# Delta inverse in a two-block kernel: the innermost level moved to VectorE, first phases as 64x64 tiles, bias rows, modulation and a table load moved

## The chip, the cores and the metric

One core of one Trainium2 chip. The time is that of one execution on the device, in microseconds. The kernel before ran three times: 841.18, 842.73 and 843.54, median 842.73. The profiled execution took 843.59. The profile calls the engines PE (TensorE's matmuls), PEld (its weight loads), DVE (VectorE), ACT (ScalarE), POOL (GpSimd) and SP (the engine that issues most DMAs).

## The reference

256 tokens of width 1024 pass through two blocks. The first is a gated delta-rule layer and an attention layer with shared keys and values. The second is a retention layer and a chunked attention layer, each with shift, scale and gate vectors (the "modulation") made from a condition vector. The change sits in the delta rule and around it. Cut to that:

```python
# per head, tokens in 4 chunks of 64
decay = exp(where(tril, g[:, None] - g[None, :], -inf))
a_mat = where(strict, (k * beta) @ k.T * decay, 0)         # 64 x 64, strictly lower
sol   = triangular_solve(a_mat + eye(64), [v * beta, k * beta * exp(g)])
# then a scan over the chunks: v_new = u - w @ state; o = q_dec @ state + qk @ v_new; ...
# second block: mod = silu(c) @ ada_w + ada_b ;  h = rms_norm(x) * (1 + scale) + shift
# attention: bias[h, i, j] = table[h, clip(i - j)]  added to the scores
```

## The kernel before, in words

**Weights.** All weight matrices stream in as 112 chunks of 1 MB (128 x 8 x 256 fp32) into three buffers `raw`. ACT rounds each half chunk to fp32r (`high`, tile `whi`), DVE makes the remainder (`low`, tile `wlo`), and PE multiplies three times per tile: high x high, high x low, low x high. One such job of 48 matmuls makes 256 output columns; the jobs are numbered J. SP loads chunk c once DVE has split chunk c - 3.

**The delta inverse.** Two chunks of 64 tokens lie side by side in a 128 x 128 matrix, so 8 heads make 16 matrices (`nt` holds minus a_mat, transposed). The inverse of each unit triangular matrix is built level by level, from blocks of 1 to blocks of 64 (`LEVELS` is 7, levels 0 to 6). The 32 x 32 blocks on the diagonal stand in `tt32`, their transposes in `uu32`. A level below 5 has two phases on PE: `first_products` (off-diagonal part times left inverse, into PSUM), an ACT copy of the result into `xs32`, and `second_products` (right inverse times that). Then DVE's `take_rows` writes the new entries into `tt32` with `copy_predicated` under the mask `lmask` and transposes the whole into `uu32`. Each phase is 64 small fp32 matmuls, 16 matrices times four 32 x 32 tiles, and a fp32 matmul runs as two records with a weight load each. Level 5 joins blocks of 32 (`take_halves`), level 6 joins blocks of 64 with 64 x 64 tiles and then transposes the 16 matrices.

**The order around it** is written out by hand on every engine. On PE, jobs 8 to 15 of the first projection are cut into `parts`, and a level lv takes this form: first products, a few transposes, `parts(J, 0, 4)`, second products, `parts(J, 4, 8)`, with J = 9 + lv. Four parts are 24 matmuls. The parts are meant to run while ACT and DVE work on a level. Each engine takes its instructions strictly in order and waits on semaphores (`t_ok` for a finished level, `x_ok` and `xc_ok` for the first phase and its copy, `u_ok` for the copies of level 6).

**The modulation.** `pair_sums(n)` on DVE multiplies a 1 MB piece `ada_ring` by the condition vector in eight passes; PE then sums over the partitions (`ada`), and DVE adds the bias (`mod_of_slot`, `take_mod`). SP loads the next piece when the one before is used up. `pair_sums(0)` stands on DVE in level 5, behind `low(15)` and ahead of `take_halves`.

**The bias rows.** POOL writes two small tables 32 times each into DRAM (`bias_rows_d`, 1 MB, and `bias_rows_b`, 512 KB), to read them back skewed as attention bias tiles. The sources `fd` and `fb` lie in `early`, memory that the outputs `ohi` and `olo` take over, so DVE waits for both writes (`scr_out`) before the delta outputs.

**The start.** ACT squares the input, then loads the table set for Ln and Exp (`ln_exp_set`), splits chunk 0 and computes the first norm. PE runs dummy matmuls (`keep_warm`) in the meantime.

## Time and profile before

| what | value |
|---|---|
| runs | 841.18, 842.73, 843.54 us; median 842.73 |
| profiled execution | 843.59 us, of which the profile's span is 841.7 |
| PE busy | 813.3 us, 97% |
| PEld / DVE / ACT / POOL busy | 791.7 / 601.6 / 488.8 / 41.1 us |
| chain that ended last | PE 83%, DVE 7%, DMA 4%, ACT 3%, issue 2% |
| PE jobs of 48 matmuls, one matmul with 256 columns | x1024 at 283 to 288 ns, overlapped |
| instruction queue | 60 packets, 0.98 MB |

A busy PE is one with a matmul in flight, so the 97% leaves some 28 us in which it had none. An idle time is put down to what ended it; "issue" means that the engine waited for nothing that the profile shows. All times in the rows are microseconds from the start of the span, unless marked ns.

### The profile page before, as it was taken

Reading aid. Unit: us, or ns where it says so; the run is one execution under the profiler, and the core shown is the slowest. Engines: PE = TensorE matmul, PEld = TensorE weight load, DVE = VectorE, ACT = ScalarE, POOL = GpSimd, SP = SyncE. Lnnn points to the kernel's source line nnn. Section 1 sums busy time; section 2 is a strip of 40 time slices with the busy share of each in tenths; the row PEclk is TensorE's granted clock in tenths of the full one; section 3 lists DMA queues with packets and bytes.
Section 4 is the critical chain, followed back from the end, with each engine's and each line's share of the span. In section 5 each row is a group of like instructions: output and inputs, shape, how many; then the busy total and the mean of one; then the engine's idle time right before and its main releaser. Section 6 shows DMA issues by size and latency. Waiting matters only on the chain.

```text
span 841.7 us, 18018 instructions
## 1 busy us (share of the span) xinstructions
PE 813.3 (97%) x7646; PEld 791.7 (94%) x7646; DVE 601.6 (71%) x1045; ACT 488.8 (58%) x762; POOL 41.1 (5%) x63
## 2 busy tenths in 40 slices
PE   7999989699999999999999999999999999999998
PEld 7899979689999999999999999999999999999998
DVE  4786865478898787796888895655777877565662
ACT  5756547355665665664444454347777767777731
POOL 0500000006300000000000000200000000000000
PEclk9999999799999999999999999999999999999999
DMA  7362236642976664467666673892465444444450
GB/s 285 122 236 100 103 104 135 144 151 77 266 270 231 239 219 165 149 216 280 207 229 239 232 259 141 213 288 102 166 235 201 167 174 160 151 152 150 150 176 26
DMA packets 26495, 153.82 MB, mean 183 GB/s; under 512 B 2848, under 2 KB 3376, under 8 KB 12080
## 3 DMA queue, kind: packets, MB, share of 16 engines
q1 hardware_dynamic: 24432, 146.37, 49.7%
q0 software_dynamic: 1984, 6.31, 4.2%
q8 instruction: 60, 0.98, 0.5%
q14 instruction: 19, 0.16, 0.1%
HBM read 150.04 MB, written 2.62 MB: 181 GB/s over the span
## 4 chain that ended last, share of the span: by engine, by line
PE 83%; DVE 7%; DMA 4%; ACT 3%; issue 2%; SPq 0%; DVEq 0%; ACTq 0%
PE ps L484 82%; DMA raw<-weights 4%; DVE wlo L1423 2%; ACT whi L1006 1%; PE ps L862 1%; DVE early L1490 1%; DVE early L1594 1%; DVE ada_ring L1504 1%; PE ps L714 0%; DVE hlo L1451 0%; DVE arena L1455 0%; ACT L995 0%; DVE olo L1468 0%; ACT hhi L1036 0%; ACT arena L1196 0%
## 5 line engine op out<-in xcount | busy, mean ns | idle before, releaser
L1423 DVE TENSOR_TENSOR wlo<-raw,whi 128x1024 fp32r<-128x1024 f32 x224 | 267.1, 1229 | 120.6 <-ACT whi L1006 120.6
L484 PE MATMUL ps<-hhi,whi 128*128 128x256 f32 x1024 | 295.1, 288 | 7.1 <-DVE hlo L1449 2.8
L484 PE MATMUL ps<-hlo,whi 128*128 128x256 f32 x1024 | 290.3, 283 | 1.1 <-issue 1.1
L484 PE MATMUL ps<-hhi,wlo 128*128 128x256 f32 x1024 | 290.2, 283 | 0.0
L1006 ACT ACTIVATE whi<-raw 128x1024 fp32r<-128x1024 f32 x224 | 227.5, 1055 | 87.3 <-PE ps L484 60.9
L484 PEld LDWEIGHTS ps<-hhi,whi 128*128 128x128 f32 x1024 | 196.5, 192 | 10.2 <-issue 7.9
L484 PEld LDWEIGHTS ps<-hlo,whi 128*128 128x128 f32 x1024 | 196.7, 192 | 1.8 <-issue 1.3
L484 PEld LDWEIGHTS ps<-hhi,wlo 128*128 128x128 f32 x1024 | 196.6, 192 | 0.0
L484 PE MATMUL ps<-ohi,whi 128*128 128x256 f32 x448 | 128.8, 288 | 1.4 <-DVE olo L1468 1.2
L484 PE MATMUL ps<-olo,whi 128*128 128x256 f32 x448 | 126.7, 283 | 0.0
L484 PE MATMUL ps<-ohi,wlo 128*128 128x256 f32 x448 | 126.7, 283 | 0.0
L484 PEld LDWEIGHTS ps<-ohi,whi 128*128 128x128 f32 x448 | 85.9, 192 | 2.8 <-issue 2.0
L484 PEld LDWEIGHTS ps<-olo,whi 128*128 128x128 f32 x448 | 85.9, 192 | 0.5 <-issue 0.5
L484 PEld LDWEIGHTS ps<-ohi,wlo 128*128 128x128 f32 x448 | 85.9, 192 | 0.0
L484 PE MATMUL ps<-arena 128*128 128x256 f32 (+2 forms) x496 | 77.7, 308 | 4.4 <-DVE arena L1605 3.4
L484 PEld LDWEIGHTS ps<-arena 128*128 128x128 f32 (+1 forms) x496 | 70.2, 191 | 10.9 <-DVE arena L1605 3.6
L484 PE MATMUL ps<-whi,hhi 128*128 128x256 f32 x256 | 72.6, 284 | 0.0
L484 PE MATMUL ps<-whi,hlo 128*128 128x256 f32 x256 | 72.4, 283 | 0.0
L484 PE MATMUL ps<-wlo,hhi 128*128 128x256 f32 x256 | 72.4, 283 | 0.0
L1504 DVE SCALAR_TENSOR_TENSOR ada_ring<-ada_ring,sil 128x256 f32<-128x256 f32 x144 | 59.0, 480 | 0.0
L484 PEld LDWEIGHTS ps<-whi,hhi 128*128 128x128 f32 x256 | 49.0, 192 | 0.7 <-issue 0.4
L484 PEld LDWEIGHTS ps<-whi,hlo 128*128 128x128 f32 x256 | 49.0, 192 | 0.3
(227 smaller groups left out, 953.7 us busy)
## 6 DMA issues: line engine op xcount, KB each, us to landing
raw<-weights SPq DMA_DIRECT2D x112, 1024.0 KB, 4.9
ada_ring<-ada SPq DMA_DIRECT2D x24, 1024.0 KB, 5.1
arena<-bias_rows_d POOLq DMA_DIRECT2D x4, 512.0 KB, 14.9
x<-x_t SPq DMA_DIRECT2D x2, 512.0 KB, 4.6
bias_rows_d<-early POOLq DMA_DIRECT2D x1, 1024.0 KB, 12.0
arena<-bias_rows_b POOLq DMA_DIRECT2D x4, 256.0 KB, 8.0
arena<-bias_rows_d POOLq DMA_DIRECT2D x4, 256.0 KB, 17.2
out_t<-x SPq DMA_DIRECT2D x4, 256.0 KB, 2.4
```

Source lines behind the costliest of these rows:

```text
L484: return pe.matmul(o, l, r, start=start, stop=stop, skip_group_check=skip)
L862: m = pe.transpose(turned_bank(hh, soft0)[:, a * P:a * P + P], ts[:, hh, c0:c0 + P], ident)
L1006: act.activation(whi[:, unit % UNITS, :, :], raw[:, c % RAW, 4 * half:4 * half + 4, :], ACT.Copy).then_inc(hi_ok_sem, 1)
L1423: dve.tensor_tensor(wlo[:, unit % UNITS, :, :], raw[:, c % RAW, 4 * half:4 * half + 4, :], whi[:, unit % UNITS, :, :].bitcast(F32), ALU.su ...
L1490: m = dve.scalar_tensor_tensor(out=dst[:, t, c0:S], in0=bank(J)[:, t, 0:S - c0], scalar=col("conv", 4 * tile + j), in1=dst[:, t, c0:S], op ...
L1504: own(dve.scalar_tensor_tensor(out=b, in0=b, scalar=sil[:, k:k + 1], in1=ring[:, :, k - 2, :], op0=ALU.mult, op1=ALU.add))
L1594: m = dve.copy_predicated(T, lmask[block_of(i), lv, :].rearrange("p (a b) -> p a b", b=n), ps[2 + i][block_of(i), 256:512].rearrange("p (a ...
```

## The change

It has six parts.

1. **Level 0** has no matmuls any more. With blocks of 1 the new entries are entries of `nt` itself, so DVE copies the superdiagonal of every 2 x 2 block into `uu32` (`next_to_diagonal`, two calls), and one transpose makes `tt32`. POOL prepares `uu32` instead of `tt32` and makes level 0's mask from the identity.
2. **First products of levels 1 to 4** run on two 64 x 64 tiles instead of four 32 x 32 tiles. For that ACT copies the 32 x 32 diagonal blocks of `nt` into a zeroed tile `ntm` (`own_blocks`), and its copies into `xs32` become two of 64 partitions instead of four of 32.
3. **Level 5 and the modulation.** On DVE `pair_sums(0)` and `take_halves` go ahead of `low(15)`, and `mod_of_slot(0)` comes into level 5. On PE `ada(0)` moves from level 6 into level 5.
4. **Bias rows.** `bias_rows_b` is written after the copies of level 6 (`u_ok` 4) instead of after level 4. The table `fd` moves from `early` into `turns`, and `bias_rows_d` is written only after ACT's sines in the second layer. DVE's wait for the writes moves behind the first output's product and waits for `bias_rows_b` alone.
5. **Table load.** `ln_exp_set()` moves ahead of the wait for the input.
6. **Keep-warm.** 20 and 12 dummy matmuls instead of 16 and 8.

```diff
+        ntm = A(16384, 16, 64)
...
-        fd = early[0:16, 0:512]
+        fd = turns[0:16, 0:2, :].rearrange("p a b -> p (a b)")
...
-                pool.tensor_copy(tt32[block_of(i), :, :], ident[block_of(i), block_of(i)].unsqueeze(1).to_broadcast([32, 16, 32])).then_inc(tt_ok_sem, 1)
+                pool.tensor_copy(uu32[block_of(i), :, :], ident[block_of(i), block_of(i)].unsqueeze(1).to_broadcast([32, 16, 32])).then_inc(tt_ok_sem, 1)
             pool.wait_ge(tt_ok_sem, 4)
-            pool.wait_ge(conv_ok_sem, 1)
+            pool.memset(ntm[:, :, :], 0.0).then_inc(ntm_zero_sem, 1)
             pool.tensor_copy(tt[:, :, :], ident.unsqueeze(1).to_broadcast([P, 16, P])).then_inc(tt_ok_sem, 1)
...
-            pool.dma_start(fd[:, 127:384], rel_d).then_inc(rel_d_in_sem, 16)
-            pool.wait_ge(rel_d_in_sem, 16)
-            pool.tensor_scalar(fd[:, 0:127], fd[:, 127:254], 0.0, fd[:, 127:128], ALU.mult, ALU.add).then_inc(fd_ok_sem, 1)
-            pool.tensor_scalar(fd[:, 384:512], fd[:, 255:383], 0.0, fd[:, 383:384], ALU.mult, ALU.add).then_inc(fd_ok_sem, 1)
-            pool.wait_ge(fd_ok_sem, 2)
-            pool.wait_ge(t_ok_sem, 5)
-            pool.dma_start(scr_d[0:32].rearrange("p h t -> h p t"), fd[:, :].unsqueeze(1).to_broadcast([16, 32, 512])).then_inc(scr_out_sem, 16)
             pool.wait_ge(bias_sb_sem, 1)
+            pool.wait_ge(u_ok_sem, 4)
             pool.dma_start(scr_b[0:32].rearrange("p h t -> h p t"), fb[0:8, :].unsqueeze(1).to_broadcast([8, 32, 512])).then_inc(scr_out_sem, 16)
             pool.wait_ge(o_split_sem, 4)
             pool.wait_ge(pos_in_sem, 16)
...
-            pool.wait_ge(scr_out_sem, 32)
+            pool.wait_ge(scr_out_sem, 16)
...
+            pool.wait_ge(fin_rope_sem, 3)
+            pool.dma_start(fd[:, 127:384], rel_d).then_inc(rel_d_in_sem, 16)
+            pool.wait_ge(rel_d_in_sem, 16)
+            pool.tensor_scalar(fd[:, 0:127], fd[:, 127:254], 0.0, fd[:, 127:128], ALU.mult, ALU.add).then_inc(fd_ok_sem, 1)
+            pool.tensor_scalar(fd[:, 384:512], fd[:, 255:383], 0.0, fd[:, 383:384], ALU.mult, ALU.add).then_inc(fd_ok_sem, 1)
+            pool.wait_ge(fd_ok_sem, 2)
+            pool.dma_start(scr_d[0:32].rearrange("p h t -> h p t"), fd[:, :].unsqueeze(1).to_broadcast([16, 32, 512])).then_inc(scr_out_sem, 16)
+            pool.wait_ge(scr_out_sem, 32)
...
-            keep_warm(16)
+            keep_warm(20)
             sums(lambda t: xsq_a[:, 4 * (t // 2) + t % 2, :], 4, S, sq_ok_sem, lambda t: t // 2 + 1)
-            keep_warm(8)
+            keep_warm(12)
...
-            parts(9, 0, 1)
...
-            def first_products(lv, c0):
-                left = left_of(lv) if lv < 5 else lambda v: v
-                n = 16 if lv < 5 else 32
-                for m16 in range(16):
...
-                    for k, r in steps_of(lv):
-                        m = mm(ps[2 + k][block_of(r), o], nt[block_of(k), m16, block_of(r)], left(tt32[block_of(k), m16, :]), m16 == 0, True)
+            parts(9, 0, 8)
+            def first_products(lv):
+                if lv < 5:
+                    left = left_of(lv)
+                    for m16 in range(16):
+                        o = slice(16 * m16, 16 * m16 + 16)
+                        for h in range(2):
+                            m = mm(ps[2 + h][half_of(h), o], ntm[half_of(h), m16, :], left(tt32[half_of(h), m16, :]), m16 == 0, True)
+                else:
+                    for m16 in range(16):
+                        o = slice(32 * m16, 32 * m16 + 32)
+                        for k in (0, 2):
+                            m = mm(ps[2 + k][block_of(k + 1), o], nt[block_of(k), m16, block_of(k + 1)], tt32[block_of(k), m16, :], m16 == 0, True)
                 return m
...
-            def second_products(lv, c0):
-                n = 16 if lv < 5 else 32
+            def second_products(lv):
+                n, c0, rows = (16, 256, range(4)) if lv < 5 else (32, 0, (1, 3))
                 for m16 in range(16):
                     o, i = slice(c0 + m16 * n, c0 + m16 * n + n), slice(m16 * n, m16 * n + n)
-                    for _, r in steps_of(lv):
+                    for r in rows:
                         m = mm(ps[2 + r][block_of(r), o], uu32[block_of(r), m16, :], xs32[block_of(r), i], m16 == 0, True)
                 return m
-            pe.wait_ge(nt_ok_sem, 4)
-            pe.wait_ge(tt_ok_sem, 4)
-            first_products(0, 256).then_inc(tp_ok_sem, 1)
-            parts(9, 1, 8)
...
                 pe.wait_ge(t_ok_sem, lv)
+                if lv == 1:
+                    pe.wait_ge(ntm_ok_sem, 2)
...
                 else:
-                    first_products(lv, 0).then_inc(x_ok_sem, 1)
+                    first_products(lv).then_inc(x_ok_sem, 1)
...
-                if last:
+                parts(J, 0, 4)
+                if lv == 5:
                     ada(0, taken(slot_of_mod(0)))
-                parts(J, 0, 4)
...
+            ln_exp_set()
             act.wait_ge(x_in_sem, 32)
             for t in range(4):
                 act.activation(xsq_a[:, 2 * t:2 * t + 2, :], x[:, 2 * t:2 * t + 2, :], ACT.Square).then_inc(xsq_ok_sem, 1)
-            ln_exp_set()
...
+            def own_blocks(m0, m1):
+                act.wait_ge(nt_ok_sem, m1 // 4)
+                for i in range(4):
+                    c = 32 * (i % 2)
+                    m = act.activation(ntm[block_of(i), m0:m1, c:c + 32], nt[block_of(i), m0:m1, block_of(i)], ACT.Copy)
+                m.then_inc(ntm_ok_sem, 1)
+            act.wait_ge(ntm_zero_sem, 1)
+            own_blocks(0, 12)
+            own_blocks(12, 16)
             first_tap(8)
             high(10)
...
                     act.wait_ge(x_ok_sem, lv)
-                    n = 256 if lv < 5 else 512
-                    for k, r in steps_of(lv):
-                        m = act.activation(xs32[block_of(r), 0:n], ps[2 + k][block_of(r), 0:n], ACT.Copy)
+                    for h in range(2):
+                        if lv < 5:
+                            m = act.activation(xs32[half_of(h), 0:256], ps[2 + h][half_of(h), 0:256], ACT.Copy)
+                        else:
+                            m = act.activation(xs32[block_of(2 * h + 1), :], ps[2 + 2 * h][block_of(2 * h + 1), :], ACT.Copy)
                     m.then_inc(xc_ok_sem, 1)
...
-            pair_matrices(3)
             dve.wait_ge(tt_ok_sem, 4)
             dve.wait_ge(mask_ok_sem, 5)
+            def next_to_diagonal(m0, m1):
+                dve.wait_ge(nt_ok_sem, m1 // 4)
+                for i in range(4):
+                    odd = lambda v: v.rearrange("p m (a two) -> p m a two", two=2)[:, :, :, 1]
+                    m = dve.copy_predicated(odd(uu32[block_of(i), m0:m1, :]), lmask[block_of(i), 0, 16 * m0:16 * m1].rearrange("p (m a) -> p m a", a=16),
+                                            odd(nt[block_of(i), m0:m1, block_of(i)]))
+                return m
+            next_to_diagonal(0, 12)
+            pair_matrices(3)
+            next_to_diagonal(12, 16).then_inc(u32_ok_sem, 1)
+            dve.wait_ge(u32_ok_sem, 1)
+            dve.transpose(tt32[:, :, :].rearrange("p m c -> p (m c)"), uu32[:, :, :].rearrange("p m c -> p (m c)")).then_inc(t_ok_sem, 1)
             def take_rows(lv):
-                dve.wait_ge(tp_ok_sem, lv + 1)
+                dve.wait_ge(tp_ok_sem, lv)
                 n = 1 << lv
...
-            take_rows(0)
...
-                low(10 + lv)
                 if lv < 5:
+                    low(10 + lv)
                     take_rows(lv)
                 else:
                     dve.wait_ge(sil_ok_sem, 1)
                     pair_sums(0)
                     take_halves()
+                    low(10 + lv)
+                    mod_of_slot(0)
                 if lv <= 3:
                     conv(8 + lv)
             pair_sums(1)
-            mod_of_slot(0)
             for g in range(4):
-                dve.wait_ge(tp_ok_sem, LEVELS - 1 + g + 1)
+                dve.wait_ge(tp_ok_sem, LEVELS - 2 + g + 1)
                 dve.tensor_copy(uu[0:64, 4 * g:4 * g + 4, 64:P], ps[2 + g][0:64, 256:512].rearrange("p (a b) -> p a b", b=64)).then_inc(u_ok_sem, 1)
             low(16)
...
-            dve.wait_ge(scr_out_sem, 32)
...
                 own(dve.tensor_tensor(oof[:, :, :], oof[:, :, :], zt[:, 2 * i:2 * i + 2, :], ALU.mult))
+                if i == 0:
+                    dve.wait_ge(scr_out_sem, 16)
                 split_o(oof[:, :, :], 2 * i, 2).then_inc(o_split_sem, 1)
```

What the order of the instructions shows on two engines. First VectorE, from level 4's rows taken to the end of level 6. In the names `wlo` is a weight remainder, `ada_ring` the modulation's piece. Before:

```order
L1594 COPY_PREDICATED early<-lmask,ps 32x16x16 x4
L1598 STREAM_TRANSPOSE early<-early 128x512
L1423 TENSOR_TENSOR wlo<-raw,whi 128x1024 x2
L1501 TENSOR_SCALAR ada_ring<-ada_ring,sil 128x2x128 x2
L1504 SCALAR_TENSOR_TENSOR ada_ring<-ada_ring,sil 128x2x128 x6
L1513 TENSOR_TENSOR ada_sum<-ada_ring 128x256
L1605 COPY arena<-ps 32x16x32 x2
L1501 TENSOR_SCALAR ada_ring<-ada_ring,sil 128x2x128 x2
```

And in the changed kernel:

```order
L1629 COPY_PREDICATED early<-lmask,ps 32x16x16 x4
L1633 STREAM_TRANSPOSE early<-early 128x512
L1522 TENSOR_SCALAR ada_ring<-ada_ring,sil 128x2x128 x2
L1525 SCALAR_TENSOR_TENSOR ada_ring<-ada_ring,sil 128x2x128 x6
L1534 TENSOR_TENSOR ada_sum<-ada_ring 128x256
L1640 COPY arena<-ps 32x16x32 x2
L1444 TENSOR_TENSOR wlo<-raw,whi 128x1024 x2
L1547 TENSOR_TENSOR mod<-ps,columns 128x2
```

The remainders of chunk 15 moved from ahead of the sums of the modulation to behind the copy that ends level 5.

Then TensorE, the small matmuls of levels 0 to 2 with their weight parts between them left out (24 matmuls each). Rows with 32x16 write 32 rows by 16 columns. Before:

```order
L484 MATMUL ps<-early,arena 32x16 x64
...
L484 MATMUL ps<-early,arena 32x16 x64
L721 MATMUL ps<-cst,arena 128x128 x8
...
L484 MATMUL ps<-early 32x16 x64
...
L484 MATMUL ps<-early,arena 32x16 x64
L731 MATMUL ps<-cst,early 128x128 x4
```

And in the changed kernel:

```order
L489 MATMUL ps<-early,arena 64x16 x32
L728 MATMUL ps<-cst,arena 128x128 x8
...
L489 MATMUL ps<-early 32x16 x64
...
L489 MATMUL ps<-early,arena 64x16 x32
L738 MATMUL ps<-cst,early 128x128 x4
...
L489 MATMUL ps<-early 32x16 x64
```

One group of 64 is gone, and the first group of each level is 32 instead of 64. The second groups are as they were.

## Rows read from the trace of the kernel before

**Rows 1.** Page: clock in 40 slices; the instruction queue (packets, MB).
```profile
PEclk9999999799999999999999999999999999999999
...
q8 instruction: 60, 0.98, 0.5%
```

**Rows 2.** PE timeline: start us, busy us, what [idle before it <-releaser].
```profile
106.63 0.39 PE L484 MATMUL ps<-hlo,whi 128*128 128x256 f32 x1 [1.13 <-issue]
...
110.90 0.25 PE L484 MATMUL ps<-early,arena 32*32 32x16 f32 x8 [1.94 <-issue]
...
121.83 0.70 PE L484 MATMUL ps<-early,arena 32*32 32x16 f32 x62 [0.80 <-issue]
...
136.86 0.31 PE L484 MATMUL ps<-early 32*32 32x16 f32 x16 [0.34 <-issue]
...
152.38 3.25 PE L484 MATMUL ps<-arena 64*64 64x64 f32 x32 [3.36 <-DVE arena L1605]
...
159.75 3.46 PE L714 MATMUL ps<-cst,arena 128*128 128x128 f32 x15 [3.73 <-issue]
```

**Rows 3.** Windows from stall end to stall end; (x) counts records.
```profile
106.62:110.89 4.27, 2.34 (x128) 2.11 (x128) 4.20 (x9) 0.00 (x0) 0.00 (x0) 1.00 0.44 182
136.85:159.74 22.89, 15.80 (x254) 14.92 (x254) 9.49 (x18) 10.29 (x19) 1.42 (x2) 0.85 0.84 152
```

**Rows 4.** Windows: a low-clock stretch, and the two bias-row writes.
```profile
112.00:115.40 3.40, 3.40 (x18) 3.40 (x18) 1.23 (x1) 3.34 (x9) 0.00 (x0) 0.50 0.02 5
139.70:151.70 12.00, 9.31 (x185) 8.76 (x183) 6.49 (x14) 7.87 (x14) 1.38 (x2) 1.00 0.85 91
151.70:162.20 10.50, 6.10 (x45) 5.42 (x46) 0.62 (x1) 2.72 (x6) 0.00 (x0) 0.56 0.76 163
```

**Rows 5.** DMA issues landing around 139 to 163 us: KB each, us to landing.
```profile
bias_rows_d<-early POOLq DMA_DIRECT2D x1, 1024.0 KB, 12.0
...
raw<-weights SPq DMA_DIRECT2D x1, 1024.0 KB, 15.8
bias_rows_b<-early POOLq DMA_DIRECT2D x1, 512.0 KB, 21.8
```

**Rows 6.** Timeline of DVE around level 5.
```profile
146.31 1.23 DVE L1423 TENSOR_TENSOR wlo<-raw,whi 128x1024 fp32r<-128x1024 f32 x1 [5.43 <-ACT whi L1006]
...
150.93 1.39 DVE L1605 COPY arena<-ps 32x512 f32<-32x512 f32 x2
```

**Rows 7.** Groups by shape, 87 to 170: busy, mean ns | idle.
```profile
L1594 DVE COPY_PREDICATED early<-lmask,ps 32x256 f32<-32x256 uint8 x20 | 11.1, 553 | 6.9 <-PE ps L484 6.7
```

**Rows 8.** DVE timeline: the idle time ahead of pair_matrices(3).
```profile
88.17 0.43 DVE L1574 TENSOR_TENSOR arena<-arena,early 128x256 f32<-128x256 f32 x1 [2.29 <-PE ps L484]
```

**Rows 9.** Timeline of PE: tiles of three shapes.
```profile
96.62 1.26 PE L484 MATMUL ps<-early,arena 32*32 32x16 f32 x128
...
140.18 1.20 PE L484 MATMUL ps<-early,arena 32*32 32x32 f32 x64
...
166.60 2.07 PE L484 MATMUL ps<-arena,early 64*64 64x64 f32 x32
```

**Rows 10.** Start of the kernel: ACT timeline.
```profile
8.54 1.28 ACT L995 ACT_TABLE_LOAD   x1
```

**Rows 11.** The first weight load, issued at 2.1 us.
```profile
DMA to landing us min/median/max: 7.4/7.4/7.4
```

**Rows 12.** DVE timeline: last level's copies, first split of the outputs.
```profile
168.23 1.40 DVE L1633 COPY arena<-ps 64x256 f32<-64x256 f32 x4
...
185.80 0.43 DVE L1466 CAST ohi<-arena 128x512 fp32r<-128x512 f32 x1
```

**Rows 13.** SP timeline: a weight chunk's issue.
```profile
286.14 0.33 SPq L369 DMA_DIRECT2D raw<-weights  x1
```

**Rows 14.** ACT timeline: the same chunk's split.
```profile
304.14 2.00 ACT L1006 ACTIVATE whi<-raw 128x1024 fp32r<-128x1024 f32 x2
```

**Rows 15.** Window of the weight phase of the second block.
```profile
286.50:297.10 10.60, 10.60 (x87) 10.44 (x86) 9.24 (x16) 5.03 (x6) 0.00 (x0) 1.00 0.78 298
```

26 lines of the change are left out of this document (14 added, 12 removed).

## Prediction

> **What bounds the kernel now.** I read the page first. PE is busy in 97% of the span and its clock row shows 9 (full, 2.4 GHz) in all slices but one, a 7 near 150 us [rows 1]. So time can only be won where PE stands still, works at the lower clock (1.2 GHz), or does work that can be left out. Next, the PE timeline for its idle times. Of the six in these rows, four end with "issue" (1.13, 1.94, 0.80 and 0.34 us), all in levels 1 to 4. One, 3.36 us, ends with DVE's copy of level 5, and one, 3.73 us, ends with "issue" inside the transposes of level 6 [rows 2]. Together 11.3 us, all between 105 and 160 us.
>
> What is "issue" here? From the end of one such stall to the end of the next PE records 128 matmuls and 128 weight loads, 256 instructions; from 136.86 to 159.75 it records 508, two times 256 with a few waits [rows 3]. The page has 60 packets of 0.98 MB in the instruction queue [rows 1], 16 KB each. So I read these stalls as PE at the end of a block of 256 instructions with the next one not there. Between the first two stalls' ends lie 4.27 us [rows 3]: about what one block needs to come.
>
> The Trainium skill ("Runtime: NRT & Kernel Launch", Instruction fetch mechanics) says the same size, 16 KiB and 256 instructions. But it calls the cost of crossing a block mostly hidden. By that rule PE would not stop there, and moving work within the blocks would give nothing; (d) below is that case.
>
> The 3.73 us has a cause of its own. From 139.7 to 151.7 us the DMA engines are busy 85% but move only 91 GB/s, and from 151.7 to 162.2 us 76% at 163 GB/s [rows 4]: these are the two bias-row writes, 12.0 and 21.8 us from issue to landing, both issued at about 140. A weight chunk beside them takes 15.8 us [rows 5]. The instruction block that PE lacks until 159.75 is, I think, queued behind them. In the second of these windows PE's mean clock is 0.56, after the wait of 3.36 us at 149 [rows 4]. An earlier drop to 0.50, from 112.0 to 115.4 us, follows the stalls of 1.13 and 1.94 us [rows 4].
>
> **The change, part by part.**
> *Table load.* It takes 1.28 us from 8.54 [rows 10], and the first split follows at 9.83. But chunk 0 lands 7.4 us after its issue at 2.1, at 9.5 [rows 11]. So the split can start only 0.3 us earlier. **-0.3.** Four more dummy matmuls ahead of the sums lie under the input load and the squares, four behind them under the split. If this cover were gone each four would cost about 1 us: eight records, at twice the 65 ns of a tile half as wide [rows 9].
>
> *Level 0.* Its 128 records took what level 1's take, 1.26 us [rows 9]. They go: **-1.2.** DVE copies instead out of SBUF, with as many elements as one `take_rows` (4 x 553 ns [rows 7]), 2.2 us. Three quarters of it stand in DVE's idle time of 2.29 us ahead of `pair_matrices(3)` [rows 8]. The rest and one transpose follow: even with 4 us for all that they end by 93, and PE needs them at 95 (96.62 [rows 9] less what PE gains until then). ACT's eight copies of at most 0.4 us each put its next work 3 us later, which is wanted after 95 too. Both at nothing; without cover, 3 us.
>
> *First products on 64 x 64 tiles.* Four 32 x 32 tiles side by side take 1.26 us for 128 records, 32 per tile; two such tiles 1.20 us for 64 records, 32 per tile, and with twice the columns [rows 9]. So a record costs 37 to 39 ns within its tile, whatever the number of tiles and columns: the load of 32 columns sets it. On one 64 x 64 tile 32 records take 2.07 us, 65 ns [rows 9]. The new phases have 32 records in each of two tiles: 2.07 us if the tiles run side by side, 4.1 if not, and 0.6 if the number of instructions decided. I take 2.0, by the nearest shape. Four phases, 0.8 each: **+3.2** (from -2.6 to +11.4). ACT's copies go from four to two, which is hidden behind four parts.
>
> The Trainium skill ("TensorE: Matmul & The Clock Gate", LDWEIGHTS) gives a load the number of its columns over 1.2 in ns, so 53 ns for 64 columns. By it a phase would take 1.7 us and the four +1.8 instead of +3.2. The rows' 65 ns hold the 64 columns that stream too.
>
> *Instruction blocks.* I count on from a known border, eight of the 256 instructions before the end of level 2's first products [rows 2]. The dummies add 32, level 0 takes away 256 and each of the four first phases 128. Then the borders fall some 130, 150, 170 and 190 instructions into the second products of levels 1 to 4, and some 80, 100 and 120 into the first products of levels 2 to 4. Between two borders lie then always a phase's rest, four parts (24 matmuls at the 0.12 us of [rows 15], 2.9 us) and the next phase's start, 4.6 to 5.2 us, against 4.27 that a block needed. Before, one block went by in 2.3 us (4.27 less the stall of 1.94). Of the four stalls, 4.2 us, I let 0.5 remain, for blocks that meet a weight load: **-3.7.** The clock should then stay up where it was 0.50 for 3.4 us: **-1.7.** Both ends: nothing won, -5.9 in all.
>
> *Level 1's DVE work.* With PE earlier, level 2 waits for `take_rows(1)`, which ends as the parts do: **+0.2.** Two waits for weight remainders ahead of parts of levels 1 and 4, 0.2 each, go: **-0.5** with the smaller gaps beside them.
>
> *Level 5.* DVE waited 5.43 us for ACT's split of chunk 15, then did the remainders, then the sums of the modulation, and only at 150.93 the copy that level 6 needs [rows 6]. Now the sums fill that idle time and the copy waits for the second products alone, over before PE's four parts. **-3.4**, all of the wait. Behind the copy now stand the remainders of chunk 15; PE wants them only after level 6's first products and transposes, 4 us later. `ada(0)` costs PE the same in its new place.
>
> *Bias rows out of level 5.* The 3.73 us stall goes with the writes: **-3.7.** Level 6 at full clock: its first products 3.25 us [rows 2] against 2.07 for the same number of the same tile at full clock [rows 9], -1.2; the transposes 3.46 us and the one before the stall, 3.9 in all, half of which would be 2.0, but the third and fourth group wait for ACT to empty a bank, 2.5: -1.4. **-2.6.**
>
> *The writes in their new places.* `bias_rows_b` starts when level 6's copies end (168.23 + 1.40 before [rows 12]), and DVE wants it landed at the first `ohi`, at 185.80 [rows 12]: 16.2 us. Alone it should take what it took behind the other, 21.8 - 12.0, 9.8 us, and 1 us of issue. Covered by 5 us; at the full 21.8 it would cost 5.6. `bias_rows_d` moves to about 287 on the old scale, where the DMA engines are busy 78% of the time [rows 15], and holds them for some 11 us. A chunk issued there at 286.14 is split only at 304.14, 18 us later [rows 13, 14]. With 3.5 us for its load (1 MB at 298 GB/s [rows 15]) and 11 behind the write it comes in time, with 3.5 us to spare. Nothing; at the worst bound, no slack at all, 11.
>
> **Sum.** -0.3 - 1.2 + 3.2 - 3.7 - 1.7 + 0.2 - 0.5 - 3.4 - 3.7 - 2.6 = -13.7 us. The profiled execution took 843.6 (span 841.7 and 1.9 around it), so it would take 829.9; it stands 0.9 above the median of the runs. From that median: **829.0 us**, 1.6% faster.
>
> **The rivals.** (a) *Stalls at new borders.* 4.6 to 5.2 us between borders is not much above 4.27, and the page shows no price for a block that meets a chunk's load. If half of the stalls come back, +2, with a drop of clock +1.7: 833. Chance 0.2.
> (b) *The 64 x 64 tiles do not run side by side*: +8.2 on the four phases, 837. Against it: tiles of 32 on the diagonal do run side by side [rows 9]. Chance 0.07.
> (c) *The write of `bias_rows_b` comes late* and takes the 16 us cover away: +5.6, 834.6. The 21.8 us of [rows 5] speak for it, that half of them was queueing against it. Chance 0.08.
> (d) *The "issue" stalls are not fetches of instructions, or are not moved by this.* Then PE's stalls have another cause and stay, the 3.73 with them. Left are -0.3 - 1.2 + 3.2 + 0.2 - 0.5 - 3.4 = -2.0, and perhaps 1 of the clock's: 840, on the border of no change. The change doesn't do what it says. Against it: the counts of 256 [rows 3]. Chance 0.04. The Trainium skill's rule above ("Runtime: NRT & Kernel Launch", Instruction fetch mechanics) would have it so.
> (e) *Slower: `bias_rows_d` starves the weights.* At 78% busy for 10.6 us [rows 15] the write leaves a backlog of 8 us. If the chunks behind it, with a modulation piece of 1 MB among them, had none of the slack read above, PE would wait 11 us, and at 0.5 clock for 10 us afterwards lose 5 more: +16, 845. It decides from 14 us of waits up. Chance 0.03.
> My forecast holds the other 0.58, with 826.5 to 831.5 as its own range: the tile phases at 1.7 or 2.3 us, no stall left or one more.
>
> **How the numbers follow.** The range takes the forecast and rivals (a) and (c), and most of (b): 825.5 to 836. It leaves out half of (b), and (d) and (e). About 0.3%, 2.5 us, is what a measurement of this kernel can tell from no change. Faster: all but (e) and two thirds of (d), 0.93. Same: 0.04. Slower: 0.03.
>
> **What the changed profile would show.** Blocks: no "issue" wait above 0.5 us between 95 and 160 us. The clock row: 9 in every slice. Tiles: a group of 64 records 64x16 in 1.7 to 2.1 us. Level 5: no wait of PE for the copy, first products of level 6 at about 144. Writes: 10 to 12 us to landing for `bias_rows_b`, no DVE wait ahead of the first `ohi`; and no PE wait for `wlo` between 270 and 300. The output jobs start 13 to 15 us earlier than at 187. I would be wrong above all if a block of instructions took longer than 5 us beside a weight load, or if the second write met a stretch in which PE has no chunk in hand.

## The result, and the profile after

The changed kernel ran at 831.88, 833.37, 833.93 and 846.60 us, the kernel before beside it at 841.18 to 846.23. The ratio is 0.9883, with a 95% interval of 0.986 to 0.9906: 1.2% faster. The ratio leaves out the run of 846.60, which is more than 1.5% above the fastest of its kernel, and the ratios of experiments 1, 2, 3 and 7 leave out seven such runs in all, so they flatter those kernels. Experiments 8 to 12 look for the cause of such runs. The profiled execution took 833.37, its span 831.5, against 841.7: 10.2 us less, where the sum had 13.7.

First the page: the clock in 40 slices, the instruction queue, the chain.

```profile
PEclk9999999999999999999999999999999999999999
...
q8 instruction: 58, 0.95, 0.5%
...
PE 84%; DVE 7%; DMA 4%; ACT 3%; issue 1%; SPq 0%; DVEq 0%; ACTq 0%
```

The 7 of [rows 1] is gone and "issue" has gone from 2% to 1%. Next the PE timeline of the changed kernel at the places of [rows 2] and [rows 9] (start us, busy us, what, idle time before it and what ended it):

```profile
96.68 2.04 PE L489 MATMUL ps<-early,arena 64*64 64x16 f32 x64
...
110.11 0.38 PE L489 MATMUL ps<-hhi,whi 128*128 128x256 f32 x1 [0.58 <-DVE early L1511]
...
119.44 0.58 PE L489 MATMUL ps<-early,arena 64*64 64x16 f32 x14 [0.33 <-issue]
...
146.94 2.08 PE L489 MATMUL ps<-arena 64*64 64x64 f32 x32
...
150.28 0.93 PE L721 MATMUL ps<-cst,arena 128*128 128x128 f32 x6 [0.25 <-ACT arena L1204]
...
174.76 0.36 PE L489 MATMUL ps<-ohi,whi 128*128 128x256 f32 x1 [0.77 <-DVE olo L1489]
```

Of the "issue" stalls one of 0.33 us is left. A new first phase takes 2.04 us. Level 6 begins at 146.94 with no wait for DVE's copy, and its first products take 2.08 us instead of 3.25. The output jobs begin at 174.76 instead of 187.10.

But these rows of the same timeline are new, and so are two windows with a granted clock of 0.50 (the lower level, 1.2 GHz). A window row gives its length, the busy time with records of PE, PEld, DVE, ACT and POOL, the clock, the DMA share and GB/s:

```profile
43.96 1.05 PE L489 MATMUL ps<-ones,early 128*128 128x1 f32 x8 [0.42 <-ACT early L1102]
45.65 0.35 PE L489 MATMUL ps<-hhi,whi 128*128 128x256 f32 x1 [0.63 <-DVE wlo L1444]
...
555.58 2.07 PE L489 MATMUL ps<-arena,ones 128*128 128x256 f32 x4 [1.58 <-ACT arena L1061]
```

```profile
46.50:49.90 3.40, 3.40 (x18) 3.40 (x18) 3.40 (x8) 0.67 (x2) 0.00 (x0) 0.50 0.65 214
555.10:558.50 3.40, 2.92 (x9) 2.55 (x10) 0.04 (x1) 1.21 (x3) 0.00 (x0) 0.50 0.50 207
```

In the first window PE got through 18 records where it does 31 at full clock (experiment 1): 13 matmuls of 0.12 us, some 1.5 us lost.

Where the time went can be read by laying the two traces side by side at the same weight matmul, the n-th of 5376, and taking start after less start before:

| stretch | difference at its end, us | moved by | forecast |
|---|---|---|---|
| start, to job 0 | -0.38 | -0.38 | -0.3 |
| jobs 0 to 4 | +1.45 | +1.83 | 0 |
| levels 0 to 4, to the middle of job 14 | -2.01 | -3.46 | -3.7 |
| levels 5 and 6, to job 15 | -12.37 | -10.36 | -9.7 |
| the rest, nearly all of it at job 72 (560 us) | -10.2 | +2.1 | 0 |

So the forecast terms came to -14.2 us against -13.7, and 4.0 us were lost in two places where the prediction had nothing.

### The profile page after: what moved, and what is told of

Same layout as the page of the kernel before. It is cut to its first block, busy times and chain, and to the rows that moved or that the text cites. A ratio compares the mean times of both kernels' runs of the same rounds, so it can differ in the third digit from the quotient of the medians.

```text
span 831.5 us, 17292 instructions
## 1 busy us (share of the span) xinstructions
PE 814.4 (98%) x7278; PEld 793.7 (95%) x7278; DVE 603.0 (73%) x1049; ACT 486.6 (59%) x761; POOL 43.6 (5%) x68
## 4 chain that ended last, share of the span: by engine, by line
PE 84%; DVE 7%; DMA 4%; ACT 3%; issue 1%; SPq 0%; DVEq 0%; ACTq 0%
PE ps L489 83%; DMA raw<-weights 4%; DVE wlo L1444 3%; ACT whi L1013 1%; PE ps L869 1%; DVE early L1629 0%; DVE hlo L1472 0%; DVE arena L1476 0%; DVE early L1511 0%; DVE arena L1511 0%; DVE arena L1652 0%; DVE ada_ring L1525 0%; DVE olo L1489 0%; ACT hhi L1043 0%; PE ps L738 0%
## 5 line engine op out<-in xcount | busy, mean ns | idle before, releaser
L1444 DVE TENSOR_TENSOR wlo<-raw,whi 128x1024 fp32r<-128x1024 f32 x224 | 267.7, 1232 | 113.8 <-ACT whi L1013 113.8
L489 PE MATMUL ps<-whi,hhi 128*128 128x256 f32 x256 | 72.6, 284 | 0.0
```

The source lines that it names most:

```text
L489: return pe.matmul(o, l, r, start=start, stop=stop, skip_group_check=skip)
L1444: dve.tensor_tensor(wlo[:, unit % UNITS, :, :], raw[:, c % RAW, 4 * half:4 * half + 4, :], whi[:, unit % UNITS, :, :].bitcast(F32), ALU.su ...
```

## The experiments

Each ratio compares with runs of the kernel before on the same chip. There were three chips: one for experiments 1 to 4 (median of the kernel before 843.7 us), one for 5 to 8 (844.1) and one for 9 to 12 (845.65). A time set against one of another experiment group is therefore less sure than a ratio.

**1. The fill of `ntm` and `tt` moved off VectorE's remainders.** Of the new rows, the one at 45.65 us waits for `wlo`. DVE's and POOL's timelines of the changed kernel there:

```profile
36.19 4.06 DVE L1444 TENSOR_TENSOR wlo<-raw,whi 128x1024 fp32r<-128x1024 f32 x2 [1.82 <-ACT whi L1013]
```

```profile
35.83 0.96 POOL L425 MEMSET arena<- 128x1024 f32 x1
36.85 2.31 POOL L426 COPY arena<-cst 128x2048 f32<-128x2048 f32 x1
```

Two remainders take 2.36 us elsewhere; here 4.06, beside POOL's fill. The edit lets the fill wait for VectorE:

```diff
             pool.wait_ge(tt_ok_sem, 4)
+            pool.wait_ge(lo_ok_sem, 10)
             pool.memset(ntm[:, :, :], 0.0).then_inc(ntm_zero_sem, 1)
```

> The changed kernel, with POOL's fill of ntm and tt held back until VectorE has split chunk 4 (about 51 us). Theory 1 (shared path of POOL and VectorE): in the changed kernel the fill at 35.8 to 39.2 us made one wlo remainder on VectorE 2.92 us instead of 1.21, TensorE therefore waited 0.42 and 0.63 us at 43.6 and 45.0, and the granted clock fell to 0.50 from 46.5 to 49.9, which cost 1.5. It expects: that remainder back at 1.2 us, both waits and the low clock gone, TensorE 2.5 us ahead of the changed kernel by 60 us, and 0.5 to 2.5 us of it left at the end (831 to 833), because at 554 us the weights arrive no sooner and the wait there grows. Rival (VectorE's chain of convolution and norms would have made TensorE wait at 43.6 us in any case): less than 1.2 us ahead at 60 us, and the clock falls all the same; end as the changed kernel.

Measured: ten runs, six at 831.29 to 833.36 and four at 841.37 to 844.49; ratio 0.9893 (0.9856 to 0.993). DVE's timeline and the window of the low clock, now:

```profile
36.23 2.36 DVE L1445 TENSOR_TENSOR wlo<-raw,whi 128x1024 fp32r<-128x1024 f32 x2 [1.82 <-ACT whi L1014]
```

```profile
46.50:49.90 3.40, 3.40 (x31) 3.40 (x30) 3.40 (x7) 0.63 (x1) 2.80 (x2) 1.00 0.70 241
```

The remainders are back at 2.36 us, the wait of 0.42 is gone, that of 0.63 stays at 0.62, and the clock held. The theory of a path that POOL and VectorE share holds for the remainders. PE was 1.80 us ahead of the changed kernel at 48 us, less than the 2.5 expected, and 1.5 of it is the clock: up to the wait at 45 us the edit had won only 0.3. For the rest the rival was right, since VectorE's chain makes PE wait there in any case. That the fill brought the low clock is not shown: experiment 2 has both waits (0.43 and 0.63) and no low clock at 46 us. In the times the gain is too small to tell: the medians of the lower groups are 832.2 here and 833.4 for the changed kernel.

**2. Work for PE in the wait at 554 us.**

```diff
                 for t in range(n):
+                    if warm and t == n - 2:
+                        keep_warm(warm)
...
-            x_sums(3)
+            x_sums(3, 6)
             keep_warm(8)
```

> The changed kernel, with six dummy matmuls before the last two terms of the norm's sums at about 554 us, where TensorE waited 1.58 us for ACT's square and the clock was then at 0.50 from 555.1 to 558.5. Theory: that fall is a consequence of the wait and of the few small matmuls ahead of it, and costs 1.7 us; with dummies in the wait the clock stays at 1.00, and the time falls by 1.5 to 1.9 us against the changed kernel (about 831.7). The wait itself is covered with work but not shortened. Rival (the clock falls for another reason, or the dummies delay the sums): same time as the changed kernel or 0.5 us more.

Measured: six runs at 832.54 to 835.31, four at 842.83 to 845.34; ratio 0.9919 (0.9878 to 0.9959). PE's timeline, and the window round it:

```profile
556.36 1.50 PE L489 MATMUL ps<-ones 128*128 128x128 f32 x12
557.70 1.03 PE L489 MATMUL ps<-arena,ones 128*128 128x256 f32 x4
```

```profile
72.60:76.00 3.40, 3.40 (x16) 2.81 (x15) 1.11 (x4) 2.24 (x4) 0.00 (x0) 0.51 0.47 200
110.20:113.60 3.40, 3.38 (x16) 3.39 (x17) 2.23 (x2) 3.37 (x9) 0.00 (x0) 0.50 0.16 22
550.00:560.00 10.00, 10.00 (x82) 9.79 (x81) 4.84 (x8) 4.60 (x6) 1.86 (x2) 1.00 0.68 265
```

At 550 to 560 us all went as the theory said: no idle time, clock 1.00, and 1.4 us gained against the changed kernel between jobs 71 and 72. But as much had been lost in jobs 69 to 71, where PE waited for weights, so the stretch as a whole gave nothing. Experiment 1 lost 1.3 us in the same jobs and was 2.3 us ahead again behind the wait, with no low clock there. This loss does not follow from a lead: here PE was 1.0 us behind the changed kernel, in experiment 1 2.0 ahead, and the profile of experiment 10, 1.0 ahead, lost nothing in these jobs. And two low stretches stood at 72.6 and 110.2 us, in code that this edit does not touch and where the changed kernel's profile had none. The time did not fall. A low stretch that one profile shows is thus not a fixed cost: over the same instructions it stands in one profile and not in another.

**3. Both edits together.**

> The two edits together. Theory: the gain of the later fill (0.5 to 2.5 us) and of the held clock (1.7 us) add up: 829.3 to 831.5, with the clock at 1.00 in every stretch. Rival (the weights bound the kernel at 554 us, so that every gain ahead of it is lost): no better than the dummies alone, about 831.7.

Measured: three runs at 832.42 to 833.42 and seven at 842.18 to 845.07; ratio 0.9935 (0.9888 to 0.9982). The profile had a low stretch at 73.2 us, again elsewhere. Neither the sum of the gains nor its absence can be told from three lower runs. The upper group was the finding here, and led to experiments 8 to 12.

**4. The bias rows written where they were, the rest as changed.**

```diff
-        fd = turns[0:16, 0:2, :].rearrange("p a b -> p (a b)")
+        fd = early[0:16, 0:512]
...
+            pool.dma_start(fd[:, 127:384], rel_d).then_inc(rel_d_in_sem, 16)
...
+            pool.wait_ge(t_ok_sem, 5)
+            pool.dma_start(scr_d[0:32].rearrange("p h t -> h p t"), fd[:, :].unsqueeze(1).to_broadcast([16, 32, 512])).then_inc(scr_out_sem, 16)
             pool.wait_ge(bias_sb_sem, 1)
-            pool.wait_ge(u_ok_sem, 4)
...
+            dve.wait_ge(scr_out_sem, 32)
```

> The changed kernel with its bias rows written where they stood before (bias_rows_d after level 4, bias_rows_b behind it, VectorE's wait for both ahead of the first delta output, table fd in early). Theory (instruction fetch queued behind the writes): in level 5 or 6 TensorE waits 2 to 4 us for nothing that the profile shows while the writes run (about 137 to 160 us), and the clock may fall behind it for another 0 to 2.6 us; time 3 to 6.5 us above the changed kernel, 836.5 to 840. Rival (the borders of the instruction blocks have moved, so that no fetch falls into the writes, and the stall of before went with levels 0 to 4): within 1 us of the changed kernel. Rival 2 (VectorE's wait for bias_rows_b ahead of the outputs is what costs): a wait of VectorE at 165 to 170 us instead, under 2 us.

Measured: median 839.64, ratio 0.9971 (0.994 to 1.0001). PE's timeline in level 6 and the window behind it:

```profile
150.89 1.33 PE L487 MATMUL ps<-arena 64*64 64x64 f32 x10 [4.91 <-issue]
```

```profile
150.50:157.30 6.80, 6.41 (x38) 5.91 (x39) 0.00 (x0) 3.31 (x7) 0.00 (x0) 0.50 0.63 131
```

The changed kernel fetched the blocks for this place with packets at 143.11 and 146.69 us. Here POOL's write of `bias_rows_d` was running. The DMA queues from 137 to 147 us (packets, MB, share of the 16 engines):

```profile
q0 software_dynamic: 288, 1.02, 96.3%
q1 hardware_dynamic: 3, 0.01, 0.3%
```

The first is POOL's queue, the second SP's. The packets with instructions started at 148.48 and 152.62, the first 2.4 us before PE went on. From the middle of job 14 to job 15 it lost 7.3 us on the changed kernel, and its median is 6.0 above. This shows the largest part of the gain: with the writes in their old place an instruction fetch comes late. Four of the ten runs lie at 842.49 to 847.99; why is not known, and it is not the race of experiment 8, since this kernel writes `bias_rows_d` at 135 us. Rival 2 is out: DVE's wait came earlier, 13.83 us for a modulation piece behind the writes, and no second one ahead of the outputs.

**5. Only the level 5 order, on the kernel before.** Part 3 of the change alone: `pair_sums(0)`, `take_halves()`, then `low(15)`; `ada(0)` in level 5.

> The kernel before with part 3 alone (level 5's sums and halves ahead of low(15), the modulation's sums in level 5); the bias rows are written where they were. Theory 1 (the fetch comes when the writes let it): level 5's wait of 3.36 us is gone, but TensorE then reaches the missing instructions 3.4 us earlier and the packet starts no sooner, so that the stall in level 6 grows from 3.73 to about 7 us; no gain, 842.5 to 844. Theory 2 (the terms add up, as the prediction's sum had it): the stall stays at 3.7 us and the time falls by 3.4 to 839.7.

Measured: median 841.61, ratio 0.9986 (0.9955 to 1.0017). The wait of 3.36 us is gone, and PE's timeline has instead:

```profile
156.78 0.58 PE L484 MATMUL ps<-arena 64*64 64x64 f32 x3 [4.41 <-issue]
```

The stall grew only from 3.73 to 4.41 us. From the middle of job 14 to job 15 PE gained 4.4 us: 3.36 of the wait, less 0.68 of the stall, and the rest of clock (6.8 us at 0.50 instead of 10.2). Theory 1 fell, because the missing block's packet did start sooner, at 154.55 instead of 157.51. Theory 2, adding the terms, was nearer, and the measured time lies between the two. The interval takes in no change, so this rests on the profile.

**6. Eight more dummies, on the kernel before.**

```diff
-            keep_warm(16)
+            keep_warm(20)
...
-            keep_warm(8)
+            keep_warm(12)
```

> The kernel before with eight more dummy matmuls at the start (20 and 12 instead of 16 and 8), which makes 16 more matmul records and 32 more instructions ahead of everything. Theory (a stall stands at every 256th instruction, where the fetch is too late): counted in matmul records from the start of the program, the stalls of levels 0 to 3 and 6 stay where they were (records 1106, 1234, 1488, 1997 and 2251, within 3), so that in the program they stand 16 matmul records earlier; their sum changes with what they fall into, 2 to 6 us for levels 0 to 3 (4.2 before); time 841 to 845. Rival (a stall belongs to its place in the program, to a queue or a semaphore): the records are 1122, 1250, 1504, 2013 and 2267, with the same lengths.

Measured: ratio 1.0015 (0.9981 to 1.0049), no change. PE's timeline:

```profile
108.57 0.58 PE L484 MATMUL ps<-hhi,whi 128*128 128x256 f32 x1 [3.48 <-issue]
...
133.92 0.23 PE L484 MATMUL ps<-early,arena 32*32 32x16 f32 x3 [1.47 <-issue]
```

Counted in matmul records from the start of the program, the stalls stand at 1106 and 1871. In the kernel before they stood at 1106, 1234, 1488, 1997 and 2251. The steps are multiples of about 127.3, and 1871 is on the same ruler, six steps from 1106. So are 1232 in the changed kernel, 978 and 1743 in experiment 7, and 1867 in experiment 4. A step of 128 matmuls with their 128 weight loads would be a block of 256 instructions; that a few records are missing would explain the difference. The first stayed at 1106 although the program had moved by 16, so the rival is out. The others of before did not come back, not even that of level 6: its packet started at 154.43 us, and PE came to it only after level 5's wait, at 155.47. So a border is where PE can stall. Whether it does, and for how long, differed from one layout of the program to the other, and no term of the theory gave it.

**7. 32 x 32 tiles in the first products again, rest as changed.**

```diff
-                        for h in range(2):
-                            m = mm(ps[2 + h][half_of(h), o], ntm[half_of(h), m16, :], left(tt32[half_of(h), m16, :]), m16 == 0, True)
+                        for i in range(4):
+                            m = mm(ps[2 + i][block_of(i), o], nt[block_of(i), m16, block_of(i)], left(tt32[block_of(i), m16, :]), m16 == 0, True)
...
+                            for i in (2 * h, 2 * h + 1):
+                                m = act.activation(xs32[block_of(i), 0:256], ps[2 + i][block_of(i), 0:256], ACT.Copy)
```

> The changed kernel with the first products of levels 1 to 4 on four 32x32 tiles again (64 matmuls instead of 32 per phase, four copies of 32 partitions instead of two of 64; ntm is still made and not used). Theory (64x64 tiles cost work and save instruction fetches): each first phase takes 1.26 us instead of 2.04, 3.1 us less in all; the 128 more instructions per phase bring the stalls for instructions in levels 1 to 4 back, from 0.3 us to 2 to 4.5 us, with perhaps one more stretch of low clock (1.5); against the changed kernel -1 to +3, 832 to 836. Rival (the stalls depend on the position of the borders alone, not on the density): no stall over 0.5 us, 830.3.

Measured: nine runs from 830.54 to 850.91, median 841.36. PE's timeline in levels 1 to 4:

```profile
104.30 0.39 PE L489 MATMUL ps<-hhi,whi 128*128 128x256 f32 x1 [2.79 <-issue]
...
129.59 0.23 PE L489 MATMUL ps<-early,arena 32*32 32x16 f32 x3 [1.18 <-issue]
```

The stalls are back with 4.0 us, as the theory had it, for 3.1 us less work. From the middle of job 4 to that of job 14 it lost 1.2 us on the changed kernel, about what the 3.4 us of low clock behind the longer stall cost. The fastest runs of the two, 830.54 and 831.88, are near each other, but the nine runs do not fall in two groups: one is at 830.54, three at 836.06 to 839.17 and five at 841.36 to 850.91. But this profile held something larger, at 293 us, far from the edit (experiment 8).

**8. Only the moved writes, on the kernel before.** Part 4 of the change alone.

> The kernel before with part 4 of the change alone (bias_rows_b after level 6's copies, bias_rows_d after the sines, fd in turns). Theory (the writes hold up an instruction fetch): of the stalls of before, the one of 3.73 us in level 6 is gone (at most 0.5 left), those of levels 0 to 3 (1.13, 1.94, 0.80, 0.34) and level 5's wait of 3.36 us stay; level 6 runs at full clock or for 3.4 us at 0.50; 3.7 to 6.3 us faster than before, 837 to 839.5. Rival (the stall in level 6 has nothing to do with the writes): it stays, and the time with it, 843.

Measured: four runs at 850.2 to 852.65, ratio 1.0088 (1.0058 to 1.0119): slower than before by 7 us, where a gain of 4 to 6 was expected. The stall of level 6 is gone, and PE gained 3.7 us there. The loss stands at 303 us. Here are the rows of POOL, SP, DVE and PE:

```profile
284.65 0.72 POOL L469 DMA_DIRECT2D bias_rows_d<-turns  x1 [0.30 <-POOL turns L467]
```

```profile
286.30 0.38 SPq L380 DMA_DIRECT2D ada_ring<-ada  x1
```

```profile
300.94 0.62 DVE L1503 TENSOR_SCALAR ada_ring<-ada_ring,sil 128x256 f32<-128x256 f32 x2 [7.13 <-DMA ada_ring<-ada]
```

```profile
308.48 1.54 PE L864 MATMUL ps<-cst,arena 128*128 128x128 f32 x6 [5.83 <-DVE arena L1738]
```

POOL issues the write of `bias_rows_d`, SP a modulation piece 1.65 us later. DVE waits 7.13 us for the piece, its softmax stands behind, and PE waits 5.83 us for that, with 6.8 us of low clock from 306.5. The profile of experiment 7 has the same chain: write at 276.02, piece at 276.88, DVE waits 8.06, PE 6.75 and 10.2 us of low clock. It lost 10.3 us against the changed kernel between 290 and 310 us. Its queues while the write ran, 277.5 to 286.5 us:

```profile
q0 software_dynamic: 224, 0.92, 96.8%
q14 instruction: 1, 0.01, 0.2%
q1 hardware_dynamic: 13, 0.00, 0.1%
```

In the profile of the changed kernel, the same two issues:

```profile
277.19 0.72 POOL L472 DMA_DIRECT2D bias_rows_d<-turns  x1 [0.30 <-POOL turns L470]
```

```profile
277.19 0.38 SPq L383 DMA_DIRECT2D ada_ring<-ada  x1
```

There the piece came through first: DVE went on at 284.67 without a wait. The profiles of experiments 1 to 3, all of them of the lower group, show the same, with both issues at 275.16, 278.18 and 276.50 us. POOL's issue hangs on a load of `rel_d`, which POOL waited 3.5 to 5.2 us for in the three profiles. So less than a microsecond decides: at the same instant the piece is first, and 0.86 us later it lands behind the whole write. Runs of the changed kernel and experiments 1 to 3 fall in two groups, 18 at 831.3 to 835.3 and 16 at 841.4 to 846.6, with none between. The next four kernels test whether this race makes the upper one.

**9. The write of `bias_rows_d` behind the tenth piece.** After that piece, at 303 us, none is loaded until 355.

```diff
             pool.wait_ge(fd_ok_sem, 2)
+            pool.wait_ge(ada_in_sem, 160)
             pool.dma_start(scr_d[0:32].rearrange("p h t -> h p t"), fd[:, :].unsqueeze(1).to_broadcast([16, 32, 512])).then_inc(scr_out_sem, 16)
```

> The changed kernel, with POOL's write of bias_rows_d held back until the tenth piece of the modulation has landed (about 308 us instead of 277; no further piece is loaded until 355 us). Theory (a race of two transfers): where POOL issues the write less than a microsecond ahead of SP's load of the eighth piece, as in the profiles of the 32x32 tiles and of the moved writes alone (276.02 against 276.88, 284.65 against 286.30), that piece lands behind the whole write, VectorE's sums and the softmax behind them are late, TensorE stops for 6 to 7 us and its clock falls; where the load is first, as in the profile of the changed kernel, nothing happens. Runs of the changed kernel and its two relatives fell in two groups, 831 to 835 and 841 to 846. With the write after the piece the upper group is gone: all runs but a stray one at 831 to 835, median about 832.5. Rival (the upper group comes from elsewhere): about half of the runs still at 841 to 846.

Measured: six runs at 831.43 to 837.42, ratio 0.9871 (0.9836 to 0.9906). No upper group. The median, 835.4, is above the expected 832.5: the three highest have a clock of 0.990 to 0.992, and the profiled one, 837.42, shows why. It had 6.8 us of low clock at 73.9 and 6.8 at 558.6 besides that at 46.6:

```profile
73.90:80.70 6.80, 6.80 (x31) 6.15 (x30) 1.74 (x5) 3.05 (x7) 0.00 (x0) 0.50 0.26 110
```

**10. The same, with the fill of experiment 1.**

> The same held-back write, and POOL's fill of tt and ntm held back until VectorE has split chunk 4. Theory: no upper group either, and 1.0 to 2.5 us below the kernel with the write alone held back, about 831. Rival (what the later fill gives back in the first jobs is lost again to a stretch of low clock elsewhere or to late weights at 554 us): same as the write alone, within 0.5 us.

Measured: six runs at 831.17 to 835.29, median 833.8, ratio 0.9853 (0.9823 to 0.9884). No upper group. The intervals of 9 and 10 overlap; that the fill adds something is not shown by them. POOL's timeline: the write now waits for the piece, which costs nothing, since its rows are read back from 515 us on.

```profile
308.59 0.72 POOL L474 DMA_DIRECT2D bias_rows_d<-turns  x1 [33.46 <-DMA ada_ring<-ada]
```

**11. Experiment 8 with the held-back write.**

> The kernel before with part 4 of the change alone, and the write of bias_rows_d held back behind the tenth piece of the modulation. Theory: the stall of 5.83 us at 303 us and its low clock are gone, and what is left is the gain first forecast for the moved writes: no stall for instructions in level 6, 837 to 840, against 850 to 853 with the write ahead of the eighth piece. Rival (the moved writes cost elsewhere too): above 843.

Measured: nine runs at 840.81 to 843.76, ratio 0.996 (0.9932 to 0.9988). With the one wait added, the same code went from 850 to 853 down to 842: the race is what cost. But 842 is above the 837 to 840 expected, in part because the kernel before was slower on this chip: against its median of 845.65 it gains 3.7 us. Level 5's wait of 3.35 us stood, and 6.8 us of low clock behind it still halved level 6:

```profile
154.26 3.67 PE L487 MATMUL ps<-arena 64*64 64x64 f32 x32 [3.35 <-DVE arena L1608]
```

```profile
154.00:160.80 6.80, 6.54 (x46) 6.05 (x47) 3.10 (x9) 2.71 (x6) 0.00 (x0) 0.50 0.79 304
```

**12. Experiment 10 with 32 x 32 tiles.**

> The kernel with both held back, and 32x32 tiles in the first products of levels 1 to 4. Theory (as the profile of the 32x32 tiles showed it: 3.1 us less work, stalls for instructions of 2.79 and 1.18 us in its place, and a stretch of low clock behind the longer one): 0 to 2.5 us above the kernel with both held back, 831 to 833.5. Rival (the stalls are hidden where the rest runs ahead): 2 to 3 us below it, 828.5.

Measured: four runs at 831.75 to 835.86, ratio 0.9864 (0.9822 to 0.9906), against 0.9853 with 64 x 64. The same within the intervals, with stalls of 2.95 and 1.19 us in the profile. No upper group either.

With 9, 10 and 12, sixteen runs have the write behind the piece and none is above 837.42; of the 34 without, 16 are above 841, and with experiment 7 it is 21 of 43. What is shown directly: the two profiles with POOL's issue ahead have the long wait, the four with both issues at once have none, and the one added wait took about 10 us off the kernel of experiment 8. That the race also makes the upper group of the changed kernel fits all of this, but two points are open. No trace of the changed kernel from its upper group was seen. And the sixteen runs were made on another chip than experiments 1 to 3 and 7, and none of the experiments with the race ran on it; against a calmer chip speaks that the kernel before spread there from 841.24 to 852.63.

Experiment 10 is the version to keep: in its six runs it is as fast as the changed kernel at its best, and none of them is of those that gain nothing.

## Why the prediction was right, and what it missed

**The number.** The forecast was 829.0 us with 826.5 to 831.5 as its own range. The lower runs have a median of 833.4, outside that range and inside the whole one only because it took in rivals (a) and (c), and neither of them happened. So it was luck in part that the range held. The terms were good, -14.2 against -13.7, and two terms at nothing were not. The signs tell the same: level 6 began at 146.94 us where the text said 144 (its own terms give 145.0, and the 1.8 lost at the start are the rest), and the output jobs began 12.3 us earlier, not 13 to 15. By its own words the chance of faster was 0.94 and not 0.93, and (b) at 837 lies outside the range, which was said to hold most of it.

**Right for the stated reasons.** Levels 5 and 6: -9.7 forecast, -10.4 measured. Experiment 4 shows that -7.3 of it hangs on the writes. The Trainium skill ("Runtime: NRT & Kernel Launch", Instruction fetch mechanics) calls the crossing mostly hidden, and by that 4 could not have moved anything. PE stalled 4.91 us in it: the trace disagrees, and rival (d) is out.

**Level 0 to 4:** -3.7 forecast, -3.5 measured. The stalls fell from 4.2 to 0.3 us, with 0.5 allowed. Experiment 6 shows that they stand at fixed counts from the start of the program, as borders of instruction blocks would. A first phase takes 2.04 us; the forecast took 2.0 from the 64 x 64 row. The Trainium skill's rule ("TensorE: Matmul & The Clock Gate", LDWEIGHTS) gave an estimate of 1.7, and the measurement decides for the row: 64 ns for each of the 32 records in a tile, although only 16 columns stream now. Rival (b) is out. Rival (a), stalls at new borders, did not come in that size: 0.33 us, and at most 0.64 for one stall and 1.3 for all (experiment 10) in later profiles. The low clock at 112 did not come back in the changed kernel's profile, but it did in experiment 2's, at 110.2. So the -1.7 for it is a gain against the one profile of before, and not one that every execution has.

**What part 2 is worth.** The price of +3.2 and the gain in stalls were both right, and they cancel. Experiment 12 with 32 x 32 tiles is as fast (833.4 against 833.8 us in experiment 10), and so is the fastest run of experiment 7. The prediction charged and credited the two without saying that this part alone comes to nothing.

**Writes.** `bias_rows_b` landed 12.1 us after its issue, where 10 to 12 was said, and DVE did not wait for it: rival (c) is out.

**Failed: "Both at nothing", for POOL's and ACT's new work at the start.** The step on level 0 priced DVE and ACT, not POOL. It moved the copy of 2048 columns further onto DVE's remainders: 4.06 us for two instead of 2.36, where the same copy in the kernel before had made it 3.21:

```profile
36.58 3.21 DVE L1423 TENSOR_TENSOR wlo<-raw,whi 128x1024 fp32r<-128x1024 f32 x2 [1.83 <-ACT whi L1006]
```

PE was 1.2 us ahead of the kernel before at 39 us and lost that at 44 to 45 us, and 1.5 of clock behind it: +1.83 in all, counted from the 0.38 at job 0. Experiment 1, without the fill there, lost 0.9 of the 1.2 too. So by these profiles the fill itself is worth 0.3 us, and the 1.5 of the clock only in executions that have the low stretch; what brings that on is open.

**Failed: nothing after job 16.** At the norm at 554 us PE's wait for ACT's square grows from 0.28 to 1.58 us, and with 3.4 us of low clock behind it the loss is 2.1. PE comes 12.5 us earlier than before, but ACT's last split ahead of the square, which waits for weights, only 11.2 (551.76 against 562.93). It is tempting to say that PE outran the weights, since the DMA engines are 95% busy between 532 and 556 us. But they are so in the kernel before too (544 to 568), and the wait does not follow the lead. PE's rows of experiments 7 and 11, where it is only 2.6 and 2.1 us ahead of the kernel before:

```profile
565.29 1.13 PE L489 MATMUL ps<-arena,ones 128*128 128x256 f32 x4 [1.37 <-ACT arena L1061]
```

```profile
566.16 1.13 PE L487 MATMUL ps<-arena,ones 128*128 128x256 f32 x4 [1.75 <-ACT arena L1057]
```

In experiment 4, 7.0 us ahead, the wait is 0.58. Over the twelve profiles without dummies there it is 0.28 to 2.02 us. Why it differs stays open; POOL's reading of the bias rows, from 515 us on, was not moved in any run.

**Failed in the chance, not in kind: rival (e).** It had `bias_rows_d` starving what is behind it, "with a modulation piece of 1 MB among them", at +16 and a chance of 0.03. By the times it happens in about half of the executions (16 of 34) and costs about 10 us: in the two profiles that show it PE waits 5.8 and 6.8 us, and the clock does the rest. The step that failed is the cover: "A chunk issued there ... comes in time, with 3.5 us to spare". That slack was read for a chunk of weights. The piece has less: DVE takes it in order ahead of the softmax, which PE waits for. The range of 825.5 to 836 holds the lower runs alone; a forecast in two parts, near 833 and near 843, would have said more.

## What to carry to other kernels

Before moving a long transfer, list every load that may be issued within its length, and for each what stands behind it in order on the consumer. A margin of less than a microsecond in the issue order does not hold from execution to execution, and here a wait on the load's own semaphore settled the order at no cost that the runs show. A term for low clock taken from one profile is a chance, not a sum. Where the DMA engines are 95% busy, a wait for weights can differ by more than a microsecond from profile to profile, so give such a stretch a margin instead of nothing. The stalls for instructions lay on a ruler of 256 instructions from the start of the program: count where it falls when dense small matmuls are moved.

## What the runs showed of the hardware

- While POOL's write of 1 MB ran, its queue had 96.8% of the 16 DMA engines' time (experiment 7, 277.5 to 286.5 us, 103 GB/s in all), and SP's queue got 13 packets in 9 us. The Trainium skill ("DMA: Bandwidth & Descriptors", Queues, rings and completion order) has each engine go round the queues packet by packet. No such sharing was seen beside this write, neither for SP's loads nor, in experiment 4, for instruction fetches. It does not hold for every transfer: from 532 to 556 us POOL's reads had 20% and SP's weights 75% of the engines in the changed kernel.
- DVE's remainders, two inputs from SBUF, took 4.06 us for two beside POOL's memset and copy, and 2.36 without them. The first took 1.23 us, the second, which met the copy under way, 2.92. The Trainium skill's rule of an exclusive lock on a shared pair of ports ("SBUF — State Buffer", Who interferes with whom) fits: POOL's copy, which met the first, was longer too, 2.31 us instead of 1.90.
- A low stretch (a granted clock of 0.50) of 3.4 us costs about 1.5 us of weight matmuls (18 records instead of 31). Among the profiles of the changed kernel and its relatives low stretches began at 46, 73, 105, 110 and 553 to 560 us, besides those behind the long waits of experiments 4 and 7, and in experiment 1's nowhere before the end.
